# Neighbourhood attention by pairs of heads in a three-block network kernel on one Trainium2 core

## What is computed

```
v = a * sigmoid(g)                        # a, g: halves of u, 512 channels each
y = depthwise_conv(v, 31 taps) + conv_b
y_conv = silu(layer_norm(y))              # over 512 channels

s_loc = q k^T / 8 + rpb[d_row, d_col]     # 8 heads of 64; -1e30 outside 16 columns
s_ctx = q k_c^T / 8                       # 256 context tokens
p = softmax([s_loc, s_ctx])
y_attn = p_loc v + p_ctx v_c
x = x + g1 * ([y_conv, y_attn] @ w_out)
```

## Time and profile before

| | |
|---|---|
| runs | 3582.5, 3585.5, 3593.2 us; median 3585.5 |
| profiled execution | 3590.8 us, its span 3588.8 us |
| PE busy | 3315.2 us (92%) |
| DVE busy | 1517.4 us (42%) |
| ACT busy | 724.6 us (20%) |
| mean granted PE clock | 0.968 |
| attention stage | 1083.5 to 1237.2 us |
| DMA | 588 MB; 428 GB/s in the expert stage, which begins behind the router |

### The profile page before, as it was taken

How to read it: one execution, slowest core, us unless ns; L and a number is a source line. 1 busy time by engine, 2 the same in 40 slices (tenths; PEclk the granted TensorE clock), 3 DMA queues, 4 the chain that set the end, 5 groups by cost and what they waited for, 6 DMA issues and landing times. The chain is left out here.

```text
span 3588.8 us, 39726 instructions
## 1 busy us (share of the span) xinstructions
PE 3315.2 (92%) x16518; PEld 1910.8 (53%) x16518; DVE 1517.4 (42%) x2332; ACT 724.6 (20%) x1110; POOL 0.2 (0%) x4
## 2 busy tenths in 40 slices
PE   7988989999898979998989898899998999999997
PEld 3475645444355633332322322587554887877874
DVE  2563146612285632222222221536443757476662
ACT  2210232311104410000000000200521323231403
POOL 0000000000000000000000000000000000000000
PEclk9997998999998999999999999999999999999999
DMA  7201033123111049999999999222111212221210
GB/s 255 94 3 67 28 115 126 47 94 129 70 47 49 17 175 428 428 428 428 428 427 428 428 428 421 96 94 88 52 70 47 71 48 71 71 71 48 71 47 24
DMA packets 120306, 588.36 MB, mean 164 GB/s; under 512 B 8896, under 2 KB 11072, under 8 KB 95424
## 3 DMA queue, kind: packets, MB, share of 16 engines
q1 hardware_dynamic: 120128, 585.83, 40.9%
HBM read 583.72 MB, written 2.10 MB: 163 GB/s over the span
## 5 line engine op out<-in xcount | busy, mean ns | idle before, releaser
L454 PE MATMUL ps<-hT,weight_ring 128*128 128x512 f32 x1216 | 545.4, 606 | 28.1 <-ACT hT L593 8.8
L454 PE MATMUL ps<-work,weight_ring 128*128 128x512 f32 (+1 forms) x960 | 422.1, 588 | 18.2 <-PEq L2514 8.3
L454 PEld LDWEIGHTS ps<-hT,weight_ring 128*128 128x128 f32 x1216 | 233.1, 194 | 317.2 <-issue 306.2
L454 PEld LDWEIGHTS ps<-work,weight_ring 128*128 128x128 f32 x960 | 179.5, 192 | 214.2 <-issue 203.5
L2087 PE MATMUL ps<-weight_ring,work 128*64 128x512 f32 x944 | 214.3, 597 | 32.2 <-DMA weight_ring<-in_w_up 18.2
L326 DVE TENSOR_TENSOR work<-work,ps 128x512 f32<-128x512 f32 x196 | 134.8, 688 | 250.9 <-PE ps L441 246.3
L441 PE MATMUL ps<-weight_ring 128*128 128x256 f32 x896 | 202.7, 379 | 0.0
L2217 DVE SCALAR_TENSOR_TENSOR xT<-ps,mod,xT 128x512 f32<-128x512 f32 x128 | 96.1, 751 | 226.1 <-PE ps L2105 223.7
L441 PE MATMUL ps<-hT,weight_ring 128*128 128x256 f32 x704 | 167.4, 396 | 19.6 <-DVE hT L602 15.6
L441 PEld LDWEIGHTS ps<-weight_ring 128*128 128x128 f32 x896 | 169.7, 190 | 24.7 <-issue 1.9
L2087 PE MATMUL ps<-work 128*64 128x512 f32 x672 | 153.3, 598 | 16.3 <-DMA work<-in_w_up 14.9
(11 more groups left out here) (365 smaller groups left out, 4188.1 us busy)
## 6 DMA issues: line engine op xcount, KB each, us to landing
weight_ring<-in_w_gate SPq DMA_DIRECT2D x34, 2048.0 KB, 40.3
weight_ring<-in_w_down SPq DMA_DIRECT2D x28, 2048.0 KB, 40.3
work<-in_w_up SPq DMA_DIRECT2D x27, 2048.0 KB, 38.9
weight_ring<-in_w_up SPq DMA_DIRECT2D x25, 2048.0 KB, 38.2
work<-in_w_down SPq DMA_DIRECT2D x21, 2048.0 KB, 40.3
weight_ring<-in_w_in_odd SPq DMA_DIRECT2D x20, 2048.0 KB, 7.8
weight_ring<-in_w_in SPq DMA_DIRECT2D x18, 2048.0 KB, 9.1
work<-in_w_gate SPq DMA_DIRECT2D x15, 2048.0 KB, 40.2
```

What stands on the lines that cost most here:

```text
L454: ins = pe.matmul(bank[0:m, 0:f], w[:, k, where:where + m], src[:, k, 0:ntok], start=k == 0, stop=k == kt - 1)
```

## The change

The unit becomes a pair of heads and 128 queries, 16 pairs, handled by a new class `PairAttention` (`Attention` stays for the other two stages that use it). The scores of the two heads alternate between array rows 0 to 63 and 64 to 127, the value products between the two halves of the output partitions. Score banks are one set for two heads in place of two sets for one. On ACT the context copies of pair i+1 now come first in the turn, ahead of the two copies and two exponentials. There are four score buffers a head, in `hT`, the spare slot and slot 11. Four bias tables have room; the first two are loaded in the projection before, once its norm is done. The pieces of the convolution norm stand ahead of the attention's part of their turn, and are spread over turns 0 to 7; PE waits in turn 7 for the root only.

```diff
+    def score(self, pe, i):
+        if i < self.N:
+            u = self.pairs[i]
+            if i >= 1:
+                pe.wait_ge(self.softened.sem, self.softened.at(2 * i))
+                if u["plain"]:
+                    pe.wait_ge(self.plain_scaled.sem, self.plain_scaled.at(2 * i))
+            for c0, n in u["keys"]:
+                for a in range(2):
+                    ins = pe.matmul(self.score_banks(a)[:, c0:c0 + n], u["q"][a], u["k"][a][:, c0:c0 + n], start=True,
+                                    stop=True)
...
+    def turn(self, pe, i, a):
+        if 0 <= i < self.N:
+            pe.wait_ge(self.normed.sem, self.normed.at(2 * i + a + 1))
+            if 2 * i + a >= 1:
+                pe.wait_ge(self.copied.sem, self.copied.at(2 * i + a))
...
+    def values(self, pe, i):
...
+            for t in range(n):
+                for a in range(2):
+                    ins = pe.matmul(self.ch.ps[64 * a:64 * a + 64, self.value_bank + g % 2, u["col"]:u["col"] + P],
+                                    u["v"][a][t], self.pT[2 * (i % 2) + a][:, t * P:(t + 1) * P], start=t == 0,
+                                    stop=t == n - 1)
...
+    def tensor(self, i):
+        def part(pe):
+            if i == 0:
+                self.score(pe, 0)
+            self.score(pe, i + 1)
+            self.turn(pe, i - 2, 0)
+            self.values(pe, i - 3)
+            self.turn(pe, i - 2, 1)
+        return part
...
+    def vector(self, i):
+        def part(v, dve):
+            if i < self.N:
+                u = self.pairs[i]
+                v.after(self.scores, i + 1)
+                if i >= 4:
+                    v.after(self.turned, 2 * (i - 3))
+                if u.get("prepare"):
+                    u["prepare"](v, dve)
+                for a in range(2):
...
+                for a in range(2):
+                    if u["plain"]:
+                        v.after(self.plain_scaled, 2 * i + a + 1)
...
+            if 1 <= i < self.N + 1:
+                j = i - 1
+                for a in range(2):
...
+                    v.after(self.expd, 2 * j + a + 1)
...
+    def scalar(self, i):
+        def part(line, act):
+            if i == 0:
+                self.scale_plain(line, act, 0)
+            self.scale_plain(line, act, i + 1)
+            for a in range(2):
+                j = i - 2
+                if 0 <= j < self.N:
+                    n = self.pairs[j]["cols"]
+                    line.after(self.turned, 2 * j + a + 1)
+                    if j >= 2:
+                        line.after(self.summed, j - 1)
+                    line(act.copy(self.pT[2 * (j % 2) + a][:, 0:n], self.turn_banks()[:, 0:n]), self.copied)
+                if i < self.N:
+                    x, stat = self.S[2 * (i % 4) + a][:, 0:self.pairs[i]["cols"]], self.st[:, 2 * (i % 3) + a, :]
+                    line.after(self.taken_max, 2 * i + a + 1)
+                    line(act.activation(x, x, ACT.Exp, bias=stat[:, 1:2], scale=-1.0, accum_out=stat[:, 2:3]), self.expd)
+        return part
...
-    def conv_made(pe):
-        pe.wait_ge(made.sem, made.at(4))
-    convolution = {0: (total, None, centre), 1: (None, square, None), 3: (square_total, take_root, scale),
-                   5: (None, finish, None), 8: (conv_made, None, None)}
+    def conv_rooted(pe):
+        pe.wait_ge(rooted.sem, rooted.at(1))
+    convolution = {0: (total, None, None), 1: (None, None, centre), 2: (None, square, None), 3: (square_total, None, None),
+                   4: (None, take_root, None), 5: (None, None, scale), 6: (None, finish, None), 7: (conv_rooted, None, None)}
     beside = Beside()
     for i in range(att.turns):
+        beside.add(-1, *convolution.get(i, ()))
         beside.add(-1, att.tensor(i), att.scalar(i), att.vector(i))
-        beside.add(-1, *convolution.get(i, ()))
...
+    def load_tables(sp):
+        norm.wait(sp, KD - 1)
+        for h in range(2):
+            sp.dma_start(ch.slot(10).rearrange("p a t -> p (a t)")[:, h * 896:(h + 1) * 896],
+                         ch.A["rpb"][:, h * 896:(h + 1) * 896]).then_inc(loaded.sem, 16)
+            loaded.total += 16
+            sp.wait_ge(loaded.sem, loaded.total)
...
-    project(ch, 5, tiles, vector_after=conv_taps(ch, vpad, y), norm=norm)
+    project(ch, 5, tiles, vector_after=conv_taps(ch, vpad, y), norm=norm, extra_sync=load_tables)
```

More of the change, by code:

```diff
@@ L1753, in finish @@
                              scale=ch.v("conv_ln_g_2", j)), made)
-    return (total, square_total), (square, take_root, finish), (centre, scale), made
+    return (total, square_total), (square, take_root, finish), (centre, scale), root
 def neighbourhood_attention(ch, y):
@@ L1773, in load @@
             loaded.total += 16
             sp.wait_ge(loaded.sem, loaded.total)
[L1776 to L1783, removed]
-        for s in range(4):
[L1785 to L1792, removed]
@@ L1793, in neighbourhood_attention, with prepare, close @@
-    att = Attention(ch, units, HD ** -0.5, bank=0, width=2, room=ch.slot(9, 2))
-    (total, square_total), (square, take_root, finish), (centre, scale), made = conv_norm(
+    pairs, both = [], (slice(0, 64), slice(64, 128))
+    for j in range(4):
+        def prepare(line, dve, j=j):
+            for h in (2 * j, 2 * j + 1):
+                line.after(loaded, 16 * (h + 1))
+                t = tab[h % 4].rearrange("p (r c) -> p r c", c=64)
+                line(dve.tensor_tensor(t, t, ch.m("win")[:, 0:64].unsqueeze(1).to_broadcast([P, 14, 64]), ADD))
+        def close(line, dve, ps, sig, j=j):
+            line(dve.tensor_copy(out[:, j, :], ps), sig)
+        for s in range(4):
+            c0 = (6 - 2 * s) * 64
+            pairs.append(dict(
+                q=[q[rows, j, s * P:(s + 1) * P] for rows in both], k=[k[rows, j, :] for rows in both],
+                keys=[(0, 512), (512, 256)], bias=[tab[(2 * j + a) % 4][:, c0:c0 + 512] for a in range(2)], biased=512,
+                plain=(512, 256), cols=768,
+                v=[[v[:, t, (2 * j + a) * HD:(2 * j + a + 1) * HD] for t in range(6)] for a in range(2)],
+                col=s * P, close=close if s == 3 else None, prepare=prepare if s == 0 else None))
@@ L1795, in neighbourhood_attention @@
+    att = PairAttention(ch, pairs, HD ** -0.5, 0, 2, [ch.hT[:, :, :].rearrange("p k t -> p (k t)"), ch.spare[:, :], ch.slot(11).rearrange("p k t -> p (k t)")], 768)
+    (total, square_total), (square, take_root, finish), (centre, scale), rooted = conv_norm(
         ch, y, ch.slot(5), ch.slot(6), 7)
[L1797 to L1800 removed]
+    def conv_rooted(pe):
+        pe.wait_ge(rooted.sem, rooted.at(1))
```

76 lines of the change are left out of this document (69 added, 7 removed).

## The result

The changed kernel takes 3561.2 us in the median of four runs (3555.1 to 3563.3); the kernel before, run beside it, 3586.5. The ratio is 0.9925 with a 95% interval of 0.9905 to 0.9944, that is 20 to 34 us saved. Forecast were 3560.5 us and 3550 to 3577. The profiled execution took 3560.3 us (span 3558.5), against 3590.8 before: 30.5 less.

A forecast was written before the change was run, and what follows sets the result against it. PE bounds the attention stage; pairing makes DVE the bound, its terms summing to 125.6 us against 153.7. Less 3 us for the clock, 25 are saved: 3565.8 profiled, 5.3 lower as median, 3560.5 us, range 3550 to 3577.

The forecast's parts named there:

- The bound that was not taken for the values, 5.84: PE in the steady part: 5.84 us per pair if only the value products don't run side by side.
- The bound of 7.2 to 7.5: PE in the steady part: 7.2 to 7.5 us per pair if nothing runs side by side.
- The row with four column groups: Expert-stage profile row: 32 matmuls of 128 columns in 1.95 us, taken as evidence that value products run side by side.
- It fits with 0.2 us to spare: Steady turns: the engines' order allows the 5.18 us period, with 0.2 us to spare on ACT, 0.6 on PE.
- The sum along DVE: Attention stage: start 8.8, pairs 76.0, norm, prepares and closes 14.7, waits 12.6, end 13.5; together 125.6 us against 153.7.
- The end: Stage's drain, from the last bias operation to the closing copy through the one transpose buffer: 13.5 us.
- partly at the low clock: Turn 4: DVE waits 4.0 us as the sum of squares stands before the scores on PE, partly at the low clock.
- after each such hole I take a few us at the low level, 1 to 1.5 us lost each: 3 us: Later prepares and turn 7: PE's idle holes lower its clock, costing 3 us in all.
- in the first five turns PE has slack even so: First five turns: PE has slack even at the low clock, where a pair takes it 8.55 us; no extra clock cost booked.
- Rival 1: PE's clock stays low 17 us at each hole, costing 14 us in place of 3; 3571.5 us, chance 0.14.
- Rivals 2 and 3: Values don't run side by side, 3566 us, chance 0.13; nothing runs side by side on PE, 3581 us, chance 0.06.
- rival 4: PE stuck at 1.2 GHz through the stage, which takes 164 us; kernel slower at 3595.5 us, chance 0.04.

The follow-up runs named there:

- run 6: Changed kernel with PE waiting until the first head's six value products have landed before the second head's; stage 138.1 us against 124.9.
- run 5: Changed kernel with PE waiting until the first head's two score products have landed before the second head's; stage 145.8 us against 124.9.
- run 4: Changed kernel with ACT's two context copies moved from the head of its turn to its end; stage 152.4 us against 124.9.
- run 3: Changed kernel with the first two bias tables loaded at the start of the stage, not in the projection before; stage 129.8 us against 124.9.
- run 7: Changed kernel with the convolution norm's pieces back where the kernel before had them, behind the attention's part; stage 129.6 us against 124.9.
- run 8: Changed kernel with 11 unread 128x512 products filling PE's waits in turns 0 to 2; stage 122.6 us against 124.9.
- run 10: Changed kernel with earlier table prepares and first scores, later Silu and scaling, plus six unread products in turns 1 and 2; stage 112.8 us, median 3549.7.
- run 12: Repeat of the kernel of run 10 beside the changed kernel on one chip; 3547.3 us, stage 112.80.
- run 11: The changed kernel again, unaltered, beside the kernel before on one chip; 3558.7 us, ratio 0.9919, stage 124.95.
- run 2: Changed kernel with both scores and values of a pair issued head by head; stage 131.3 us against 124.9.
- run 1: Changed kernel with only the value products of a pair issued head by head, not alternating; stage 131.3 us against 124.9.
- run 9: Changed kernel with earlier table prepares and first scores, later Silu and scaling, no fillers; median 3545.4 us, ratio 0.9888, stage 115.7.

## Why the prediction was right, point by point

**The bound.** "The steady period goes from 7.48 to 5.18 us, with DVE the bound": 5.13 measured. PE's 4.54 us per pair (1.48 + 0.80 + 1.46 + 0.80) came out as 1.49, 0.80, 1.46, 0.80. The bound that was not taken for the values, 5.84, is near to what run 6 gives when it forbids it, 6.13; serial scores give 6.17 (run 5). The bound of 7.2 to 7.5, with nothing side by side, no run tested. Added up from runs 5 and 6 it would be 7.7 us, an estimate.

**Values beside each other.** The Trainium skill, page "TensorE: Matmul & The Clock Gate", section "The mechanism", has weight loads overlap running matmuls only where the row group differs; from this the prediction had worked out 5.84 us per pair. The trace disagrees: 24 records, each with weights of its own, in 1.46 us with all rows in use in both heads, and that is what one head took before. The row with four column groups was the better guide.

**ACT.** "It fits with 0.2 us to spare": in the steady turns ACT waits 0.2 and 0.4 us, about 0.6 per pair (5.18 less 4.62 would be 0.56), and DVE never waits for it. Run 4 shows that this depends on the place of the context copies; the count of the prediction holds for this order alone.

**The sum along DVE.** To the end of the first bias 8.9 us (8.8 forecast). Work from there to the end of the last bias, 89.8 (76.0 + 14.7 = 90.7). Waits 11.0 (12.6): turn 3 0.28 (0.8), turn 4 2.15 (4.0), turn 5 1.61 (1.6), turn 6 1.44 (1.0), turn 7 5.53 (5.2). The end 15.2 (13.5). Together 124.9 against 125.6. The early load of the tables, costed at nothing, did cost nothing: from the projection's first load of weights to the stage's first matmul it is 180.3 us in the kernel before and in run 3, which do without it, and 180.2 and 180.3 in the changed kernel's two executions.

The mis-sized terms are two. In turn 4 the sum of squares was taken "partly at the low clock"; it ran at the full one, four matmuls of 512 columns in 3.5 us:

```profile
1107.57 3.60 PE L1877 MATMUL ps<-work,masks 128*128 128x512 f32 x8
1111.10 1.56 PE L1542 MATMUL ps<-work 64*128 64x512 f32 x8
```

The end was 1.7 us too short. The drain is a chain of single steps through the one transpose buffer, each waiting for the other engine; the timeline of PE:

```profile
1197.10 0.88 PE L1553 MATMUL ps<-masks,spare_slot 128*128 128x128 f32 x6
1199.00 0.84 PE L1553 MATMUL ps<-masks,spare_slot 128*128 128x128 f32 x6 [1.02 <-ACT spare_slot L1636]
1199.77 1.53 PE L1567 MATMUL ps<-spare_slot,work 128*64 128x128 f32 x24
```

**The clock.** The mechanism of the prediction held but for this term: the step "after each such hole I take a few us at the low level, 1 to 1.5 us lost each: 3 us" failed. PE idled 1.72 and 2.75 us at the two later prepares and its clock did not fall, and DVE waited for nothing behind them:

```profile
1150.58 1.56 PE L1542 MATMUL ps<-work 64*128 64x512 f32 x8 [1.72 <-DVE hT L1594]
1174.08 1.56 PE L1542 MATMUL ps<-work 64*128 64x512 f32 x8 [2.75 <-DVE hT L1594]
1175.57 0.88 PE L1553 MATMUL ps<-masks,hT 128*128 128x128 f32 x6
```

It was low in three stretches, from 1090.8, 1124.9 and 1142.0 us, for 13.7, 6.8 and 3.4 us: 24 us against 34 before, all of them in turns 1 to 7. That was no rule: in runs 3, 7, 8, 10 and 12 a stretch of 3.4 us at the lower level did follow the last prepare, behind the same hole of 2.75 us, and in the changed kernel's second execution (run 11) again none did. Run 8's timeline of PE, to be held against the last two rows above:

```profile
1171.98 1.98 PE L1545 MATMUL ps<-work 64*128 64x512 f32 x8 [2.75 <-DVE hT L1600]
1173.89 1.54 PE L1556 MATMUL ps<-masks,hT 128*128 128x128 f32 x6
```

Even there DVE went on without a wait, so in run 8 such a fall cost nothing. The other half of that step, "in the first five turns PE has slack even so", failed as well, as run 8 shows, and the other way: at least the 1.4 us of turns 3 and 4. The 3 us for the clock were thus booked in the wrong turns; in the sum of 125.6 turn 4 had been walked "partly at the low clock", so a part of what the early turns cost is in the 12.6.

**The sum.** 28.8 us were saved in the stage, 28.1 forecast for it without the clock and 25 with it. The medians differ by 25.3. The stage itself, 124.9 us, is 3.7 under the forecast's 128.6 and just under the 125 to 132 that the prediction gave as its sign. That 3560.5 and 3561.2 agree so well is luck: two errors cancel. The profiled execution was forecast at 3565.8 and took 3560.3, 5.5 less (3.7 in the stage, 1.6 around it). The prediction then took off 5.3 us for the median, as the kernel before had it, but here the median lies 1.0 above the profiled execution, 6.3 the other way.

**Rivals.** Rival 1 (a clock that stays down 17 us at each hole) didn't come; the longest stretch was 13.7 us, the later ones 6.8 and 3.4. Rivals 2 and 3 are excluded by the value and score groups. For rival 4 the clock would have to stay low through the stage; it was low for 24 of 124.9 us.

**The parts of the change,** by the runs: scores side by side 21 us, values 13, context copies ahead 27.5, the early tables 4.9, the norm in pieces 4.7. They don't add up to 28.8 and needn't: each is what is lost when it alone is taken away, with the clock's part in it (low for 44 us in run 5, 51 in run 4), and several of them are the same period seen from different engines. No run took away scores and values side by side together; if their 21 and 13 us added, the stage would be 159 us, longer than before.

## What to carry to other kernels

Where two independent products each use half of the array, measure whether they run together before counting on one rule: here the row halves did in either order of issue, the column halves fully only when alternated. Once an engine is relieved, count a whole turn on every other engine, in the order of its queue; one group of copies in the wrong place cost nearly as much as the whole change brought. And a turn in which DVE never waits can still be followed by a wait that comes from PE's slow clock two turns earlier, so test by filling the holes, not by arguing from who is idle.

## What the runs showed that I had not expected

- Row halves: with the second head's products issued behind all of the first's, both still started 13 ns apart, and the pair took 1.50 us (run 2). With a wait between them 3.10 us (run 5).
- Column halves: 1.46 us for six products of each head when alternated, 2.38 when issued by head, 3.04 with a wait (runs 1 and 6).
- With eleven and six useless products PE was at the full clock over the first turns, and the stage was 2.3 and 2.9 us shorter (runs 8 and 10; in run 8 0.9 us of it may not be theirs).
- PE idle for 2.7 us at a prepare was followed by a fall of the clock in some executions (the last prepare in runs 3, 7, 8, 10 and 12, the one before it in runs 9, 10 and 12) and not in others (the last one in the changed kernel, twice, and in run 9), with the same turns around it.
- The stage repeats within 0.1 us, while the 1080 us ahead of it took 1074.8 us in run 4 and 1080.7 in run 8, with the same work in them.
